# The feed-forward of a two-group encoder layer by Strassen's algorithm in two halves through DRAM, the second matrix's token sums formed by GpSimd

## The reference, cut to what matters

```
h = rmsnorm(x, norm_ffn)
x = x + jnp.square(jax.nn.relu(h @ w_ffn1)) @ w_ffn2     # w_ffn1 1024 x 4096, w_ffn2 4096 x 1024
y = rmsnorm(x, norm_final)
```

## Time and profile before

| | |
|---|---|
| time, median of 3 runs | 1810.17 us (1808.38 to 1810.33) |
| the profiled execution, its own time | 1809.99 us |
| its span (first to last instruction) | 1808.0 us |
| granted TensorE clock, mean | 0.993 |
| TensorE matmul busy | 1753.9 us, 97% |
| VectorE busy | 942.9 us, 52% |
| ScalarE busy | 689.5 us, 38% |
| GpSimd busy | 34.1 us, 2% |

### The profile page before, as it was taken

The page is one execution under the profiler, slowest core; times in us unless marked ns, Lnnn a source line. Parts: engine busy times, 40 slices in busy tenths (PEclk is TensorE's granted clock), DMA queues, the critical chain, the costliest instruction groups (busy, mean ns, idle before and its releaser), DMA issues. The chain is left out here.

```text
span 1808.0 us, 24870 instructions
## 1 busy us (share of the span) xinstructions
PE 1753.9 (97%) x10398; PEld 1563.6 (86%) x10398; DVE 942.9 (52%) x1307; ACT 689.5 (38%) x986; POOL 34.1 (2%) x49
## 2 busy tenths in 40 slices
PE   9999999999999989999989999999999999999998
PEld 8777777889999978789878989889898989899896
DVE  6577778566776798454455433333233332323334
ACT  5577777653443565123553311112030211211122
POOL 1000000000000001000000000000000000000001
PEclk9999999999999989999999999999999999999999
DMA  5322122110111243612430111111111111111102
GB/s 184 91 64 75 47 75 75 48 49 24 49 54 31 72 149 103 229 47 71 120 103 24 59 47 36 36 57 37 47 41 30 59 36 47 44 39 36 47 24 105
DMA packets 147936, 118.02 MB, mean 65 GB/s; under 512 B 4593, under 2 KB 129137, under 8 KB 147826
## 3 DMA queue, kind: packets, MB, share of 16 engines
q1 hardware_dynamic: 147826, 116.44, 20.9%
HBM read 98.40 MB, written 18.02 MB: 64 GB/s over the span
## 5 line engine op out<-in xcount | busy, mean ns | idle before, releaser
L227 ACT ACTIVATE sbuf_w_hi<-sbuf_raw 128x1024 fp32r<-128x1024 f32 x116 | 121.7, 1053 | 379.6 <-PE PS L2193 315.5
L2147 PE MATMUL PS<-sbuf_h_hi,sbuf_w_hi 128*128 128x384 f32 x768 | 256.9, 334 | 0.0
L2149 PE MATMUL PS<-sbuf_h_hi,sbuf_w_lo 128*128 128x384 f32 x768 | 256.6, 334 | 0.0
L2148 PE MATMUL PS<-sbuf_h_lo,sbuf_w_hi 128*128 128x384 f32 x768 | 256.6, 334 | 0.0
L2245 DVE TENSOR_TENSOR sbuf_X<-PS,sbuf_X 128x512 f32<-128x512 f32 x144 | 99.5, 691 | 251.6 <-PE PS L2193 251.4
L2192 PE MATMUL PS<-sbuf_w_hi,sbuf_u_lo 128*128 128x512 f32 x576 | 227.2, 395 | 0.0
L2193 PE MATMUL PS<-sbuf_w_lo,sbuf_u_hi 128*128 128x512 f32 x576 | 227.2, 395 | 0.0
L2191 PE MATMUL PS<-sbuf_w_hi,sbuf_u_hi 128*128 128x512 f32 x576 | 227.2, 394 | 0.0
L567 PE MATMUL PS<-sbuf_h_hi,sbuf_w_hi 128*128 128x384 f32 x600 | 212.7, 355 | 6.1 <-ACT sbuf_g_N L578 2.7
L569 PE MATMUL PS<-sbuf_h_hi,sbuf_w_lo 128*128 128x384 f32 x600 | 202.5, 338 | 0.0
L568 PE MATMUL PS<-sbuf_h_lo,sbuf_w_hi 128*128 128x384 f32 x600 | 202.5, 337 | 0.0
(11 more groups left out here) (269 smaller groups left out, 2867.2 us busy)
## 6 DMA issues: line engine op xcount, KB each, us to landing
sbuf_raw<-w_ffn SPq DMA_DIRECT2D x64, 512.0 KB, 4.0
sbuf_raw<-w_in SPq DMA_DIRECT2D x28, 512.0 KB, 4.8
sbuf_X<-x_prompt SPq DMA_DIRECT2D x16, 512.0 KB, 7.3
sbuf_s_cK<-cache_sb_k SPq DMA_DIRECT2D x8, 512.0 KB, 4.6
sbuf_s_cV<-cache_sb_v SPq DMA_DIRECT2D x4, 1024.0 KB, 7.9
sbuf_raw<-w_out SPq DMA_DIRECT2D x8, 512.0 KB, 4.2
out_yp<-sbuf_X SPq DMA_DIRECT2D x8, 512.0 KB, 2.6
sbuf_r_lo<-mixT SPq DMA_DIRECT2D x7, 576.0 KB, 9.1
```

Of the source, the lines that this page charges most:

```text
L227: act.activation(w_hi[s][:], raw[s % 2][:], ACT.Copy).then_inc(cut_hi[s % 2], 1)
L2147: pe.matmul(out, hi, h_hi[:, kb, tok], start=kb == 0, stop=False)
L2148: pe.matmul(out, hi, h_lo[:, kb, tok], start=False, stop=False)
L2149: last = pe.matmul(out, lo, h_hi[:, kb, tok], start=False, stop=kb == KB - 1)
```

## The change

Both matrix products of the feed-forward are done by a form of Strassen's algorithm with seven products in place of eight. The first runs over all 1152 tokens as 2 x 2 blocks: tokens in halves of 576 (HT), features in halves of 512, hidden blocks in pairs (a unit is 256 hidden columns, 16 units). The seven products of a unit use the token operands A11, A12, A22 and the sums S1 to S4, which are made once at the start, and the weight blocks B11, B21, B22, T1 to T4, of which T1 to T4 are made for every unit by VectorE (`f_blocks`, 4 instructions of 128x512). A product is two quarters of 288 tokens (QT), 4 feature blocks by 3 passes. Each product's weight is cut into a ring of 6 (`w_high`, `w_low`).

The squared hidden activations of a unit are written to a DRAM tensor uD together with the three sums that the second product needs; a fourth sum overwrites the block A21. These four sums are formed by GpSimd (`ff1_pool`), in a single buffer f_S. SP stores the unit in two DMAs (1152 KB and 768 KB). X is stored to DRAM (xD) and read back.

The second product runs over the 1024 prompt tokens only, in 4 turns of 4 units, 7 products each, and the samples are done beside it in the ordinary way. Its operands come back from uD in 1024 KB loads (`u_unit`), both operands are cut into rings of 6 pieces, and each product is added to X2 by VectorE.

The order of the first product's steps, and the waits that the prediction speaks of:

```diff
+        def ff_step(n):
+
+            if n == 0:
+                return [("P5", 0), ("P6", 0), ("P7", 0), ("P4", 0), ("P3", 0)]
+            if n == UNITS - 1:
+                return [("P6", n), ("P5", n), ("P7", n), ("P4", n), ("P3", n)]
+            return [("P6", n), ("P1", n + 1), ("P7", n), ("P2", n + 1), ("P5", n), ("P4", n), ("P3", n)]
+
+        FF = [("P1", 0), ("P2", 0), ("P1", 1), ("P2", 1)]
...
+        def ff1_act(act):
...
+            for s, (what, n) in enumerate(FF):
+                if what in ("P1", "P6", "P7", "P4"):
+                    act.wait_ge(f_p, s + 1)
+                    x = f_part(n, {"P1": 0, "P6": 2, "P7": 3, "P4": 1}[what])
+                    if what == "P1":
+                        if n >= 2:
+                            act.wait_ge(f_st[n % 2], 32 * (n // 2))
...
+                    act.activation(x, pair(what, n), ACT.Relu if what == "P4" else ACT.Copy).then_inc(f_cp, 1)
+                    if what == "P4":
+                        act.wait_ge(f_cp, CP[what, n])
+                        act.activation(x, x, ACT.Square).then_inc(x_sq.sem, 1)
...
+                w_high(act, s + RING)
...
+        def ff1_dve(dve):
...
+            def out_of(what, n):
+
+                i, ends, left = {"X11": (0, "P2", "P1"), "X22": (3, "P5", "P7"), "X12": (2, "P3", "P6")}[what]
+                dve.wait_ge(f_p, FF_AT[ends, n] + 1)
+                dve.wait_ge(f_cp, CP[left, n])
+                dve.tensor_tensor(f_part(n, i), pair(ends, n), f_part(n, i), ALU.add).then_inc(f_ev, 1)
+                dve.wait_ge(f_ev, EV[what, n])
+                if what != "X12":
+                    squared(f_part(n, i))
+                    return
+                squared(f_part(n, i)).then_inc(u_sq.sem, 1)
...
+            for s, (what, n) in enumerate(FF):
+                if outs_after(s):
+                    out_of(*outs_after(s))
...
+                if n >= 1 and n + 1 < UNITS and s == FF_STEP[n]:
+                    f_blocks(dve, n + 1)
+                w_low(dve, s + RING)
...
+        def ff1_pool(pool):
+            for n in range(UNITS):
+                u = f_ub[n % 2]
+                a11, a21, a12, a22 = (u[:, x:x + HS] for x in (0, HS, T, T + HS))
+                pool.wait_ge(u_sq.sem, u_sq.n(n + 1))
+                pool.wait_ge(x_sq.sem, x_sq.n(n + 1))
+                if n:
+                    pool.wait_ge(f_st[(n - 1) % 2], 32 * ((n - 1) // 2 + 1))
+                pool.tensor_tensor(f_S[:, 0, :], a21, a22, ALU.add).then_inc(u_sum.sem, 1)
+                pool.tensor_tensor(a21, a11, a21, ALU.subtract)
+                pool.wait_ge(u_sum.sem, u_sum.n(2 * n + 1))
+                pool.tensor_tensor(f_S[:, 1, :], f_S[:, 0, :], a11, ALU.subtract).then_inc(u_sum.sem, 1)
+                pool.wait_ge(u_sum.sem, u_sum.n(2 * n + 2))
+                pool.tensor_tensor(f_S[:, 2, :], a12, f_S[:, 1, :], ALU.subtract).then_inc(f_u, 1)
...
+            def store_u(n):
+
+                sp.wait_ge(f_u, n + 1)
+                sp.dma_start(uD[:, n, 0:2 * T], f_ub[n % 2]).then_inc(f_st[n % 2], 16)
+                sp.dma_start(uD[:, n, 2 * T:UW].rearrange("p (a b) -> p a b", a=3), f_S).then_inc(f_st[n % 2], 16)
...
+            for n in range(UNITS - 2):
+                sp.wait_ge(w_cut_lo.sem, w_cut_lo.n(FF_AT["P3", n] + 1))
+                pair_unit(n + 2)
+                store_u(n)
```

More of the change, by code:

```diff
@@ L495, in norm_step @@
                 norm_scale(dve, n, t)
-            if t >= 1 and not n.final:
+            if t >= 1:
                 norm_low(dve, n, t - 1)
@@ L2109, in cross_dve @@
             low(NU - 1)
-        f_rl, f_hi, f_sq, f_lo, f_y, f_add = (sem("f_" + x) for x in ("rl", "hi", "sq", "lo", "y", "add"))
-        f_third = sem("f_third")
-        def ff_round(g, second):
-            return R_FF + g * 2 + second
-        LAG = 2
-        pieces = [(b, 0, 3) for b in range(FB - 1)] + [(FB - 1, g, g + 1) for g in range(3)]
-        NPC = len(pieces)
-        def piece_after(b, t):
-            return next(k for k, (b_, lo, hi) in enumerate(pieces) if b_ == b and lo <= t // 3 < hi) + 1
@@ new lines, in build @@
+        FF = [("P1", 0), ("P2", 0), ("P1", 1), ("P2", 1)]
+        FF_STEP = []
+        for n in range(UNITS):
+            FF_STEP.append(len(FF))
+            FF += ff_step(n)
+        FF_AT = {x: s for s, x in enumerate(FF)}
+        NFF = len(FF)
+        LASTU = UNITS - 1
+        f_p, f_t, f_cp, f_ev, f_u = (sem("f_" + x) for x in "p t cp ev u".split())
+        f_st = [sem(f"f_st{i}") for i in range(2)]
+        w_cut_hi, w_cut_lo = (Since(x[0], unit(R_MO + 1, 0)[1]) for x in (cut_hi, cut_lo))
@@ new lines, in build, with outs_after @@
+        copies = [x for x in FF if x[0] in ("P1", "P6", "P7", "P4")]
+        CP = {x: i + 1 for i, x in enumerate(copies)}
+        def outs_after(s):
+            what, n = FF[s]
+            if what == "P2":
+                return ("X11", n)
+            if what == ("P7" if n in (0, LASTU) else "P5"):
+                return ("X22", n)
+            return ("X12", n) if what == "P3" else None
+        outs = [outs_after(s) for s in range(NFF) if outs_after(s)]
+        EV = {x: i + 1 for i, x in enumerate(outs)}
@@ new lines, in tiles_of_product, with by_tile @@
+        def tiles_of_product(k):
+            s = ["S"] if k % 7 in WITH_S else []
+            return s + [0, 1, 2, 3] if k % 7 == 6 else [0, 1, 2, 3] + s
+        def by_tile(k):
+            return k % 7 == 1 or k == NPR - 1
+        Y, STEP = {}, []
+        n_p = NFF
+        for k in range(NPR):
+            for kb in range(GU):
+                if kb == GU - 1:
+                    for t in tiles_of_product(k):
+                        n_p += 1
+                        Y[k, t] = n_p
+                else:
+                    n_p += not by_tile(k)
+                STEP.append(n_p)
+            if by_tile(k):
+                STEP[GU * k:] = [n_p] * GU
@@ new lines, in mo_after, with mo_behind @@
+        def mo_after(act, p):
+            if p == 0:
+                w_high(act, 0)
+                w_high(act, 1)
+                return
+            norm_square(act, n_ff, 0)
+            for t in range(NT):
+                if t + 1 < NT:
+                    norm_square(act, n_ff, t + 1)
+                if t >= NT - 2:
+                    w_high(act, t - NT + 4)
+                ff_high(act, t)
+        def mo_behind(dve, p):
+            if p == 0:
+                f_blocks(dve, 0)
+                w_low(dve, 0)
+                w_low(dve, 1)
```

898 lines of the change are left out of this document (678 added, 220 removed).

## The result

The changed kernel takes 1837.37 us (median of 4 runs, 1833.42 to 1839.08) against 1810.06 us before in the same session (1808.38 to 1810.33): a ratio of 1.015, 95% interval 1.013 to 1.0169. The profiled execution is the 1833.42 us one. TensorE now stands idle for 8% of the span where it was 3%, and VectorE works a quarter more.

A forecast was written before the change was run, and what follows sets the result against it. TensorE alone was taken to bound the kernel before. 1810.0 - 84.5 (matmuls) + 12 (start) + 76 (unit chain) + 4 (second product and end) = 1817.5 us; the forecast's own range 1804 to 1838, the whole range 1741 to 1848.

The forecast's parts named there:

- Matmuls: TensorE in both products: 288-column matmuls 133.3 ns apart; 706.5 us of matmuls against 791, so -84.5 us.
- Start, +12: Before the first product: extra copies, adds and operand sums after the norms leave TensorE waiting, +12 us (6 to 18).
- A unit's chain, +76: First product: GpSimd's late sums delay store and next weight load; 28.1 us a unit against 22.7, +76 us (32 to 96).
- Clock, 0: First product: P4 at half speed ends only when X22 comes anyway, so 0; 24 to 45 us if P3 is met.
- the 12 us of joints: Both products: time between matmul products, transposes included, 803 - 791 = 12 us, taken as unchanged.
- Second product and end, +4 (0 to 12): Second product: first products wait for the last unit's X12 and the samples' cut, +4 us; tail of norms 0.
- stores hidden: Rival, first product: TensorE stays the bound, only the start and 4 us remain, 1741.5 us; chance 0.25, hidden or nearly.
- GpSimd served quickly: Rival, first product: sums done in 7.3 to 9.5 us, 2.3 to 4.5 us lost a unit, 1774 to 1804; chance 0.24.
- the low bound of 32: First product's unit chain: sums at 1.24 us each, never blocked, done at 7.3 us; 2.3 x 14 = 32 us.
- The clock rival: Rival, first product: P3 also runs at the low clock level, 1842 to 1863 us; chance 0.11, shared with VectorE first.

The follow-up runs named there:

- e1: Changed kernel with the four token sums of a unit formed by VectorE behind X12's square, in place of GpSimd; 1764.64 us, 0.9755 of before.
- e6: Changed kernel with SyncE's order changed at the passage: pieces of products 1 and 2 ahead of blocks B12 and B22, product 2's ahead of unit 15's store; 1827.51 us.
- e12: Changed kernel with one load moved: product 2's token pieces issued directly behind product 1's, ahead of X rows and unit 15's store; 1831.12 us, 1.0134 of before.
- e4: Changed kernel with the second product's pieces 4 and 5 cut later, behind the last unit's X12, on ScalarE and VectorE; 1832.37 us, 1.0135 of before.
- e7: e6 with e4's later cuts: pieces 4 and 5 cut behind the last unit's last sum on both engines; 1825.54 us, 1.009 of before.
- e2: e1 plus GpSimd forming four sums a unit on a tile nobody reads, beside VectorE's weight sums; 1797.91 us, 0.9937 of before.
- e5: Changed kernel with the next weight pair's load between the 1152 KB store and the sums' store, ScalarE waiting for the first alone; 1820.96 us, 1.0073 of before.
- e9: Changed kernel with e3's and e5's edits, and the next weight pair's load ahead of both stores on SyncE's queue; 1785.93 us, 0.9876 of before.
- e8: e7 with the four sums on VectorE, as in e1; 1750.72 us, 0.9676 of before.
- e3: Changed kernel with three of VectorE's four weight sums moved earlier, to behind P4's place, before GpSimd's sums begin; 1842.91 us, 1.0191 of before.
- e10: e9 with e7's order at the passage between the two products; 1770.00 us, 0.9791 of before.
- e11: e10 with the four sums on VectorE (e8 with e3's, e5's and e9's moves); 1785.93 us, 0.9878 of before.

## Why the prediction was right and where it was wrong

The forecast was 1817.5 us; the profiled execution took 1833.42, 15.9 more, and the median 4 more again. So a loss of 7.5 us was forecast and one of 27 measured between the medians. The direction was right, but the chance of it was put at a half only, and the near time is in part luck: the steady units were forecast some 24 us too long in all, and the clock, the late loads and the passage too short.

*Matmuls.* Right: 55 starts of 288 columns stand between 1235.80 and 1242.95 us, 132.4 ns apart, against my 133.3.

*Start, +12.* Right: in e1, where little else waits, TensorE's waits from the first P1 to P4 of unit 0 (at 1038.71) sum to 11.1 us.

*A unit's chain, +76.* The mechanism was right in the main, and the sum for it too high. The last sum was done 8.4 us behind P3's end, not 10.4: GpSimd's sum of 512 columns takes 1.29 us where VectorE is idle (at 1427.45) and 1.62 to 1.75 beside it, where I had 1.5 and 0.65 of waiting. The Trainium skill (GPSIMD Engine Reference, "3.1 Elementwise — side-by-side cycle accounting") led to 1.56 us, an estimate (its figure and the row of 1152 columns give 1.55); the measured 1.29 decides. Store landed at sum + 7.4 (I had 6.4), load at sum + 10.3 (9.9), from there to P3 4.2 (4.5), P3 itself 3.5 (3.2). A unit of 26.4 us follows, 1.7 shorter than my 28.1. One link I had only in part: the load stands not only behind the store. For ten of the thirteen such loads SyncE is free 0.1 to 0.4 us before VectorE's cut of P3's piece ends, and issues the load as it ends (at 1271.62, cut done at 1271.59); for the other three, the one shown at 1245.92 among them, SyncE is the last.

The Trainium skill (SBUF — State Buffer, "SBUF: two separate sides") has the loser of the shared ports blocked for the whole instruction. By that rule a pair of one sum each would take 1.29 + 0.69 = 1.98 us; the starts of VectorE's sums, 1237.67 and 1239.38, are 1.71 apart. The measurement decides: in this trace the two hold each other up by less than a whole instruction.

*Clock, 0.* Too low: six of the thirteen P3s of units 1 to 13 ran in part at the lower level, which made each 1.5 us longer, 9 us in all. In four of these units the load landed 1.2 us late besides; no run shows why. With both the mean unit is 27.5 us, 4.8 above 22.7 and not 5.4: 14 x 4.8 = 67 us where I had 76. Without them it would be 14 x 3.7 = 52. The errors offset each other in part. The first product took 8 us less than my terms make (358.4 + 12 + 76 + half of the 12 us of joints = 452).

*Second product and end, +4 (0 to 12).* This is the step that failed. By my terms the second product is 348.1 + 4 + 6 = 358 us; it took 383.5. That is 25 us more than my terms, on a term of 4 us whose upper bound was 12. TensorE waited 27.2 us in it, 23.2 of them at the passage, and ran 8 us at half the clock, which is 4 us lost. I had asked whether the last X12 and the samples' cut were late by their own work, and had not followed SyncE's queue through the passage, where 3 MB of blocks and the samples' columns are issued ahead of the pieces that ScalarE's and VectorE's queues stand at, and four rows and a store that waits for GpSimd ahead of the next ones. In the steady turns such a load lands in some 5.2 us (the median of all 28 in the page's list of DMA issues); with this queue ahead it took 10.5. e6 and e12 show it: changing SyncE's order alone gives 12.8 and 9.7 us of the second product back, and with e4's cuts 14.0 (e7). The other 11 us are not traced by any run; 8.9 of them are waits at the passage that e7 still has. e1 shows what is for the most part not to blame: with no GpSimd in it, the second product still took 377.5.

The Trainium skill (DMA: Bandwidth & Descriptors, "Queues, rings and completion order") says that each DMA engine takes the descriptors of one issuing engine's queue in their order. By that rule what is issued ahead counts, and what is issued behind does not; the runs agree: with 1 MB more right behind them (e12) the pieces of product 1 landed 10.5 us after their issue as before (1447.36 to 1457.88), and with 2 MB less ahead of them (e6) 14.7 us after the issue of unit 14's store in place of 20.0.

*What the forecast had left out in the first product.* e2's 33 us: a GpSimd that VectorE never waits for still holds up the VectorE cut that frees the weight buffer. In the changed kernel this way lies just beside the store's: in the unit shown the cut ends at 1245.17 and SyncE is busy issuing the store until 1245.87, and for ten of the thirteen loads the cut ends last, by 0.4 us at most. So it hardly showed in the sum; it set the bound as soon as the store was eased (e5).

*Of the rivals,* stores hidden was not the changed kernel's case; only e9's order brings a unit to 23.9 us. GpSimd served quickly was true in its numbers: the last sum at 8.4 us lies in its 7.3 to 9.5 and the 3.7 us of a unit in its 2.3 to 4.5, though neither engine kept the shared way to itself and both went at a slower pace. Its 1774 to 1804 us were missed by what the clock and the passage added. (Its lower end was set too high: 2.0 us and four sums of 1.24 make 7.0 and not 7.3, which takes 4 us off the low bound of 32.) The clock rival was true for six of thirteen units, at 1.5 us each.

How far this stands: that the 4 us wait left in e7 and e8 comes from B12 and B22 was read from the timelines, not tried. Why GpSimd's sums in e3 kept 1.74 us with VectorE idle for part of the time is open, as is why six P3s of the changed kernel, eleven in e3 and none in e9 meet the lower clock.

## What to carry to other kernels

Where two products meet, walk the issuing queue instruction by instruction with its bytes, as carefully as the steady loop: here TensorE waited 23 us in that one passage, where fourteen units' chain cost 67. Before giving an engine a side job, look at what its neighbour on the shared way has queued behind the slowed instructions, above all anything that frees a buffer. And an order of transfers is right for one timing of its producers: the same three moves took 56 us off with GpSimd's late sums (e7 to e10) and cost 35 with VectorE's early ones (e8 to e11). Before an edit is called useless, see whether the clock was the same: e3's lost 9 us to it.

## What the runs showed of the hardware that was not expected

- GpSimd's sum of two SBUF tiles of 512 columns took 1.29 us alone, and VectorE's 0.69. With both busy, each took 1.6 to 1.8, neither the sum of the two (1.98) nor its own time.
- The granted clock fell to 0.51 at six of thirteen P3s, after waits of 1.9 to 2.1 us (2.09 at 1203, 1.92 at 1285) and once of 3.37 (at 1065), while P3 at 1232 ran at the full clock behind a wait of 3.14 and P3 at 1258 behind one of 1.95.
- A store of 1920 KB let ScalarE go on 6.6 us after its issue with nothing ahead of it (e8; 6.5 to 8.7 over the units); the first 1152 KB alone took 9.8 us with a 1 MB load issued 0.4 us ahead (e11; 8.5 to 10.2).
